# Four idle products ahead of each weight entry in two of the four expert groups

## The reference

```python
a = jnp.einsum('nd,edf->nef', t, w_gate)
b = jnp.einsum('nd,edf->nef', t, w_up)
hid = jax.nn.silu(a) * b * combine[:, :, None]
routed = jnp.einsum('nef,efd->nd', hid, w_down)
shared = (jax.nn.silu(t @ w_sh_gate) * (t @ w_sh_up)) @ w_sh_down
```

## Time and profile before

| | us |
|---|---|
| median of 3 runs | 743.07 |
| lowest, highest | 741.06, 743.9 |
| the profiled execution | 743.77 |
| its span, first to last instruction | 741.9 |
| mean granted clock, share of full | 0.947 |
| PE busy in the span | 662.8 (89%) |
| third group (unrolled), from its first wait's end to the next group's | 258.6 to 318.3 |
| fourth group (in the loop) | 318.3 to 378.0 |

### The profile page before, as it was taken

The page is one execution under the profiler, slowest core; times in us unless marked ns, Lnnn a source line. Parts: engine busy times, 40 slices in busy tenths (PEclk is TensorE's granted clock), DMA queues, the critical chain, the costliest instruction groups (busy, mean ns, idle before and its releaser), DMA issues.

```text
span 741.9 us, 10752 instructions
## 1 busy us (share of the span) xinstructions
PE 662.8 (89%) x4431; PEld 516.6 (70%) x4431; DVE 334.6 (45%) x606; ACT 280.4 (38%) x521; POOL 42.9 (6%) x63
## 2 busy tenths in 40 slices
PE   8999899997895777677678999999989999999996
PEld 5979787733641133042148999989789999999994
DVE  7677555621020102012057565638845554445554
ACT  6655562311010110011045565673545433344432
POOL 1000102000000000000026400000000000000000
PEclk9999999999999687698799999999999999999998
DMA  9925309589869999999995534335525545545201
GB/s 354 417 90 223 114 1 407 245 340 388 348 251 424 420 422 421 422 419 422 420 420 208 197 114 148 137 115 174 187 106 204 182 173 197 198 170 180 105 1 57
DMA packets 26144, 182.22 MB, mean 246 GB/s; under 512 B 3040, under 2 KB 3168, under 8 KB 4464
## 3 DMA queue, kind: packets, MB, share of 16 engines
q1 hardware_dynamic: 25344, 178.81, 61.5%
q10 hardware_dynamic: 752, 2.73, 0.9%
HBM read 180.48 MB, written 1.05 MB: 245 GB/s over the span
## 4 chain that ended last, share of the span: by engine, by line
PE 67%; DMA 18%; DVE 7%; ACT 4%; issue 2%; POOL 1%; SPq 0%; DVEq 0%; ACTq 0%; POOLq 0%
PE ps L1320 64%; DMA ring<-stream_dram 17%; PE ps L1323 3%; DVE ring_r L351 2%; ACT single L344 1%; DMA vec<-small_dram 1%; DVE work L1274 1%; ACT work L746 1%; POOL stat L781 0%; DVE work L1277 0%; DVE single L1196 0%; ACT single L663 0%; DVE work L1183 0%; POOL stat L788 0%; DVE work L1230 0%
## 5 line engine op out<-in xcount | busy, mean ns | idle before, releaser
L1320 PE MATMUL ps<-turned,single 128*128 128x256 f32 (+1 forms) x1312 | 239.9, 285 | 2.0 <-DVE turned L1293 1.2
L1320 PEld LDWEIGHTS ps<-turned,single 128*128 128x128 f32 x1312 | 202.9, 189 | 4.7 <-issue 2.3
L1320 PE MATMUL ps<-turned,ring_r 128*128 128x256 f32 (+1 forms) x656 | 185.3, 282 | 0.0
L351 DVE TENSOR_TENSOR ring_r<-ring,single 128x1024 fp32r<-128x1024 f32 x134 | 160.9, 1243 | 49.8 <-ACT single L344 49.6
L1320 PE MATMUL ps<-ring,work 128*32 128x512 f32 (+2 forms) x814 | 136.1, 680 | 39.9 <-DMA ring<-stream_dram 35.6
L344 ACT ACTIVATE single<-ring 128x1024 fp32r<-128x1024 f32 x134 | 133.8, 1050 | 1.8 <-DMA ring<-stream_dram 1.2
L1320 PEld LDWEIGHTS ps<-ring,work 128*32 128x32 f32 (+1 forms) x814 | 39.7, 128 | 121.2 <-DMA ring<-stream_dram 75.0
L1320 PEld LDWEIGHTS ps<-turned,ring_r 128*128 128x128 f32 x656 | 124.0, 189 | 0.0
L1320 PE MATMUL ps<-single,turned 128*128 128x512 f32 (+3 forms) x208 | 60.1, 367 | 2.8 <-DVE turned L1007 1.8
L1320 PE MATMUL ps<-work 128*128 128x128 f32 (+5 forms) x272 | 55.7, 407 | 3.4 <-DVE work L877 1.8
L1320 PE MATMUL ps<-single 128*128 128x512 f32 (+1 forms) x257 | 51.2, 355 | 7.6 <-DVE single L1196 6.5
(11 more groups left out here) (226 smaller groups left out, 599.0 us busy)
## 6 DMA issues: line engine op xcount, KB each, us to landing
ring<-stream_dram SPq DMA_DIRECT2D x161, 1024.0 KB, 12.1
work<-stream_dram SPq DMA_DIRECT2D x5, 1024.0 KB, 13.0
turned_w<-stream_dram SPq DMA_DIRECT2D x2, 1024.0 KB, 10.8
gain<-gains_dram ACTq DMA_DIRECT2D x3, 512.0 KB, 8.6
cst<-consts_dram ACTq DMA_DIRECT2D x1, 1066.0 KB, 9.0
h<-x_dram SPq DMA_DIRECT2D x2, 512.0 KB, 3.9
out_dram<-work SPq DMA_DIRECT2D x4, 256.0 KB, 2.0
vec<-small_dram SPq DMA_DIRECT2D x1, 451.5 KB, 5.9
```

Source lines behind the costliest of these rows:

```text
L351: dve.tensor_tensor(ring_r[:, place, a], ring[:, place, a], w_hi[k % HIGHS][:, a].bitcast(F32), ALU.subtract).then_inc(s["wlo_done"], 1)
L1320: return pe.matmul(o, lhsT, rhs, start=start, stop=stop, **kw)
```

## The change

A function `keep_warm(bank)` inside `moe_group` issues four idle products (128 x 128 weights from `xh`, 512 columns from `xh`) into the given bank when the new argument `starved` is set. It is called ahead of the wait for each entry, except for the first three of a group: into bank 5 in `gate_up`, into bank 4 in `down`. `starved` is set for the third group (g = 2) and for the loop.

```diff
-            def moe_group(it, g, moe_slot, freed, first=False, after_shared=False):
+            def moe_group(it, g, moe_slot, freed, first=False, after_shared=False, starved=False):
+
+                def keep_warm(bank):
+
+                    if starved:
+                        idle_products(ps[:, bank, :], xh[:, 0, 0:P], xh[:, 0, 0:512], 4)
 
                 pe.wait_ge(s["sel_done"], it + 1)
                 if first:
@@ -1663,6 +1668,8 @@
 
                 def gate_up(p):
                     for t in range(DT):
+                        if p or t >= 3:
+                            keep_warm(5)
                         w = moe_slot(p * Q_SLOTS + t)
                         if p == 0:
 
@@ -1690,6 +1697,7 @@
                     pe.wait_ge(s["hid_done"], it * PAIRS + (p + 1))
                     for n in range(2):
                         for j in range(FF // P):
+                            keep_warm(4)
                             w = moe_slot(p * Q_SLOTS + GU_SLOTS + 2 * n + j)
                             for e in range(4):
                                 last = mm(ps[e * CAP:(e + 1) * CAP, 6 + n, :], hid[:, j, e * CAP:(e + 1) * CAP],
@@ -1733,7 +1741,7 @@
                 return ready
 
             for g in range(LOOPED):
-                moe_group(g, g, moe_slot(g) if g else first_slot, used, g == 0, g == 1)
+                moe_group(g, g, moe_slot(g) if g else first_slot, used, g == 0, g == 1, g == 2)
                 if g == 0:
                     shared_gate_up()
                     shared_turned()
@@ -1742,7 +1750,7 @@
             rounds = pe.value_load(rounds_i[0:1, 0:1], min_val=1, max_val=ROUNDS)
             with pe.Fori(LOOPED, rounds * GROUPS) as it:
                 g = pe.snap(it % GROUPS)
-                moe_group(it, g, moe_slot(it), used)
+                moe_group(it, g, moe_slot(it), used, starved=True)
```

## The result

| | before | changed | difference |
|---|---|---|---|
| median (4 runs each) | 743.18 | 753.59 | +10.4 |
| lowest to highest | 741.06 to 743.9 | 752.78 to 757.38 | |
| ratio | 1 | 1.0156 [1.0128, 1.0185] | |
| profiled execution | 743.77 | 754.0 | +10.2 |
| its span | 741.9 | 752.2 | +10.3 |

The kernel became slower, by twice what was forecast. A later set of runs of the same two kernels gave 750.75 (6 runs, 748.71 to 754.38) against 743.15 (23 runs), ratio 1.012 [1.009, 1.0151]. So the change costs 8 to 10 us.

A forecast was written before the change was run, and what follows sets the result against it. The prediction took the DMA weight stream to pace the expert stage. PE would fall 2.44 us behind per group, 4.9 over two; added to the median of 743.07 us this gave 748.0, range 742.0 to 754.0.

The forecast's parts named there:

- What bounds the kernel: Expert stage: the DMA weight stream paces it at 2.49 us an entry, hiding a low clock while entries take less.
- The price of a batch: Between expert entries: four products with both switches cost 1.12 us, an entry with its batch 1.00 + 1.12 = 2.12 us.
- the forecast's bound: Lower bound for an entry with its batch, if switches cost nothing: 0.88 + 4 x 0.23 = 1.80 us.
- rival 1: Expert stage: switches cost less, step at most 2.00 us, batches stay under the stream; 743.1 give or take 1, chance 0.25.
- The walk: PE's work over one group, never waiting for weights, at 2.4 GHz: 62.14 us against 59.70 of stream, 2.44 behind per group.
- threshold: Delay of the end by entry step: none up to 2.00 us, 2.3 at 2.06, 4.9 at 2.12, 23 at 2.56.
- The end: Behind the last expert group: nothing absorbs the delay; a late last entry makes everything behind it late, one for one.
- The cover of the ring: Weight slots reused 8 entries on: PE may lag about 11 us, largest lag 8.5, so transfers stay back to back.
- The clock: Expert stage with batches: PE never idle for long, clock 1.0 nearly throughout; a fall now costs 1.4 us per spell.
- signs of being wrong: In the changed trace: PE still waiting for landings in the last `down`, or a clock spell or DMA gap in the stage.
- Rival 2: The forecast's delay plus two to four clock spells of 1.4 us, above all around the turn: 749.5 to 754, chance 0.14.
- The median: Whole kernel: the earlier median of 743.07 us plus 4.9 of delay over two groups, 748.0.

The follow-up runs named there:

- the change once more: The changed kernel, four products per batch, run again with no edit: 750.75 us, ratio 1.012 against the kernel before.
- early batches: Against the changed kernel, the first batch of each `down` issued ahead of the wait for the transposed hidden values: 744.64 us.
- filled turns: Changed kernel plus idle work ahead of the hidden-values wait: four products 749.19 us, 8 transposes 748.89; products throughout the turn, first `down` batches ahead of their wait, 746.03.

## Why the prediction was right or wrong

**What bounds the kernel: right.** The stream paced both groups, and a faster clock inside them was worth nothing. Two and three products raised it to 0.92 to 1.00 and moved no time. Had what the low clock takes from PE come off the time, 59.7 x (0.23 + 0.17) = 23.9 us by the clock of the earlier trace rows would have been the gain; the runs with two and three products, 743.89 and 744.21 us beside 742.65, show none of it.

**The price of a batch: right.** 2.12 us per step, from the scatter's neighbourhood, was measured as 2.12, and the steps with three and eight products as 1.89 and 3.04 (275.70 to 278.74). The switch is not free: without it the step would be 1.80 us by the forecast's bound. The four products sharing one weight tile changed nothing, as the batch took 1.12 us (265.26 to 266.38), what the scatter had given: rival 1 fell on this.

**The walk: right to 0.2 us.** 62.14 us per group forecast, 62.26 to 62.31 measured at full clock. The scatter's row, the walk and the expectation of the change once more are written for 2.4 GHz, a figure that no run shows. What the profiles show is a granted clock of 1.00 over those two groups and over the scatter's row (290.78 to 293.82), and of 0.50 in the low stretches. The walk also gave a threshold at a step of 2.00 us. The runs only put it between 1.89 and 2.12: nothing at three products, a delay at four, a full slope beyond.

**The end: right.** From the last scatter on, the delay went through one for one: the second block's first transposes come 13.51 us behind it before (377.94 to 391.45) and after (385.01 to 398.52).

**The cover of the ring: nearly right.** The lag was put at 8.5 us and became 13.0 us with the falls (the fourth group's first entry at 327.05, its landing at 251.86 + 25 x 2.4875 = 314.05). That is over the 11 us allowed, and the share of 0.98 is its trace; it cost nothing visible, since PE was the bound by then.

**The step that failed is "The clock".** The sentence was: with the batches PE is never idle for long, so I expect 1.0 nearly throughout. The term was put at zero and the forecast made without it, although the prediction names a clock spell in the stage among the signs of being wrong. The profile had 13.6 us at half clock in the two groups, worth 5.9 us, and the second one 6.8 us, worth 2.8. Rival 2 had priced this rightly, at 1.4 us for a stretch and 749.5 to 754 in all, named the turn as the place, and got 0.14. The misjudgement was in the evidence. The earlier trace rows held two gaps that the clock had outlasted at 1.00, with PE busy 0.44 us in 2.00 and 0.01 in 3.20, the first of them at the very same place of a group, and I read them as a rule. They were two outcomes of something that goes either way. Of the eight groups in these profiles with four or eight products per batch and an unfilled turn, six had a low stretch that began at a turn or in the first products behind it, and two had none. (Of the two groups with early batches one had such a stretch, of the six with filled turns one.) What decides between them, no run shows. In the kernel before that chance cost nothing, because the stream covered it: 59.64 to 60.08 us a group at clocks of 0.77 to 0.83. By taking up the cover, the change made it count. So the forecast's own sentence, that a fall now costs, should have moved its centre and not only its upper end.

**The median.** 4.9 us forecast, 10.4 and 7.6 measured. Two groups at full clock are 5.2 us over the stream. The remaining 2 to 5 us are of the size of the low stretches inside them, 2.8 and 5.9 us in the two profiles; in the executions without a profile only the mean clock tells of them. The early start and the late end of the one profiled execution are within what two profiles of the kernel before differ by, and go with its low clock there; they belong to no step.

## What to carry to other kernels

Idle work that kept the clock up was free here only while the engine had slack (three products, a step of 1.89 us: no cost that the runs can tell; four, 2.12 us: 8 to 10 us). So add up a whole period of its work, with the parts that wait for nobody, and not only the one step beside its transfer: here 2.12 us under 2.49 still made a group 2.6 us longer. Before filling waits in a stage that a stream paces, ask what the faster clock would buy; here it was nothing, and the slack that was spent had been covering the falls of the clock. If it is done, put the idle work ahead of waits on other engines, where four products cost nothing (ahead of the transposes) or 0.35 us of their 1.12 (ahead of the first entry of `down`), and keep it under the slack.

## What the runs showed of the hardware that was not expected

- Between products on four column strips and products on the full array, the changed kernel shows 0.20 us more on a batch of four (1.12 where four of 44 products in a row take 0.92, at 0.23 from start to start) and 0.12 more on the entry ahead of it (1.00 where entries in a row take 0.88).
- Where PE was the bound, 1 us at half clock (0.50) cost 0.42 to 0.46 us in four groups, a little less than half.
- The clock fell from 1.00 to 0.50, for 3.4 or 6.8 us, at a turn, where PE has 3.7 us of transposes and small products with two waits (1.21 and 0.56 us), or, in the second pair, 2.0 us of transposes with waits of 0.99 and 0.47 us. It did so in some groups and not in others that were the same to 0.1 us. With 0.9 us of products in the longer wait it still fell in one group of two, with 0.9 us of transposes in none of two.
- Two profiles of the same kernel differ by 5.7 us ahead of the expert stage and by 4.9 us behind it, with 10.2 us more low clock ahead in the one and 13.3 us more behind in the other. That the spans come out alike all the same, 741.9 and 741.5, is chance as far as two profiles tell.
